# Adaptive modulation in float32 on four column quarters, with key and value products between its tiles

## The reference

```python
silu_c = jax.nn.silu(c)
silu_cc = jax.nn.silu(c_ctx)
shift, scale, gate = jnp.split(silu_c @ w_ada[l] + b_ada[l], 3, axis=-1)
shift_c, scale_c, gate_c = jnp.split(silu_cc @ w_ada[l] + b_ada[l], 3, axis=-1)
h = _modulate(_rmsnorm(xs, norm_g[l]), shift[:, None], scale[:, None])
hc = _modulate(_rmsnorm(cs, norm_g[l]), shift_c, scale_c)
pc_kv = hc @ w_l[:, OFF_K:OFF_ZA]
kc = _rmsnorm(_heads(pc_kv, 0, N_KV_HEADS), k_norm_g[l])
vc = _heads(pc_kv, KV_W, N_KV_HEADS)
p = h @ w_l
q = _rope(_rmsnorm(_heads(p, OFF_Q, N_Q_HEADS), q_norm_g[l]), cos, sin) * q_scale
k = _rope(_rmsnorm(_heads(p, OFF_K, N_KV_HEADS), k_norm_g[l]), cos, sin)
v = _heads(p, OFF_V, N_KV_HEADS)
```

## Time and profile before

| | us |
|---|---|
| Median of 3 runs (2142.15 to 2145.62) | 2142.19 |
| The profiled execution | 2143.34 |
| its span | 2141.70 |
| TensorE busy in the span | 2080.9 |
| VectorE busy | 1376.2 |
| ScalarE busy | 1093.9 |
| GpSimd busy | 48.8 |
| Granted TensorE clock, mean share | 0.987 |

### The profile page before, as it was taken

One profiled execution on the slowest core, in us unless ns is written; L12 is line 12 of the kernel. 1 busy time (PEld: TensorE's weight loads), 2 busy tenths in 40 slices (PEclk: granted clock), 3 DMA queues, 4 the chain that ended last, 5 costly groups with the idle time before them and its releaser, 6 DMA issues.

```text
span 2141.7 us, 30864 instructions
## 1 busy us (share of the span) xinstructions
PE 2080.9 (97%) x12240; PEld 1817.9 (85%) x12240; DVE 1376.2 (64%) x1788; ACT 1093.9 (51%) x1461; POOL 48.8 (2%) x59
## 2 busy tenths in 40 slices
PE   6999999999999998999999999999999999999998
PEld 4678888878889987999998788888789889997886
DVE  4755765557776656666676666666775755775554
ACT  7633455544443444444457666666455445774432
POOL 0000000000000000000000000010000000000000
PEclk9999999999999999999999999999999999999998
DMA  8852443347775554344455445445444454334552
GB/s 352 348 216 99 179 156 119 118 138 275 276 293 178 198 211 153 136 185 178 171 201 193 158 177 193 179 179 201 183 161 175 157 195 177 118 107 168 199 195 79
DMA packets 57802, 394.59 MB, mean 184 GB/s; under 512 B 6624, under 2 KB 9104, under 8 KB 10592
## 3 DMA queue, kind: packets, MB, share of 16 engines
q1 hardware_dynamic: 54240, 376.07, 48.2%
q0 software_dynamic: 2448, 15.51, 1.9%
q10 hardware_dynamic: 1008, 1.53, 0.2%
HBM read 390.92 MB, written 2.16 MB: 184 GB/s over the span
## 4 chain that ended last, share of the span: by engine, by line
PE 93%; DVE 3%; ACT 1%; DMA 1%; issue 1%; SPq 0%; DVEq 0%; ACTq 0%
PE ps L2156 13%; PE ps L2158 13%; PE ps L2157 13%; PE ps L2176 10%; PE ps L2168 9%; PE ps L2170 9%; PE ps L2169 9%; PE ps L2177 5%; PE ps L2265 1%; PE ps L2429 1%; PE ps L2407 1%; PE ps L2256 1%; PE ps L2257 1%; DMA side<-in_ctx 1%; PE ps L2616 1%
## 5 line engine op out<-in xcount | busy, mean ns | idle before, releaser
L1163 DVE TENSOR_TENSOR w_lo<-raw,w_hi 128x1024 fp32r<-128x1024 f32 (+1 forms) x660 | 795.0, 1220 | 569.1 <-ACT w_hi L489 567.4
L489 ACT ACTIVATE w_hi<-raw 128x1024 fp32r<-128x1024 f32 (+1 forms) x660 | 685.3, 1051 | 670.5 <-PE ps L2158 339.0
L2168 PE MATMUL ps<-act,w_hi 128*128 128x256 f32 x1152 | 333.3, 289 | 1.9 <-DVE w_lo L1163 1.2
L2170 PE MATMUL ps<-act,w_lo 128*128 128x256 f32 x1152 | 326.8, 284 | 0.0
L2169 PE MATMUL ps<-act,w_hi 128*128 128x256 f32 x1152 | 326.8, 284 | 0.0
L2176 PE MATMUL ps<-act,w_hi 128*128 128x512 f32 x896 | 315.2, 397 | 1.3 <-DVE side L1438 1.3
L2156 PE MATMUL ps<-w_hi,act 128*128 128x512 f32 (+1 forms) x640 | 252.1, 394 | 4.7 <-DVE act L1206 2.8
L2177 PE MATMUL ps<-act,w_lo 128*128 128x256 f32 x896 | 250.2, 279 | 0.0
L2158 PE MATMUL ps<-w_hi,act 128*128 128x512 f32 (+1 forms) x640 | 247.7, 387 | 0.0
L2157 PE MATMUL ps<-w_lo,act 128*128 128x512 f32 (+1 forms) x640 | 247.3, 386 | 0.0
L2156 PE MATMUL ps<-w_hi,gated 128*128 128x512 f32 x576 | 226.2, 393 | 2.3 <-DVE gated L1978 1.4
(11 more groups left out here) (317 smaller groups left out, 2810.8 us busy)
## 6 DMA issues: line engine op xcount, KB each, us to landing
raw<-in_tiles SPq DMA_DIRECT2D x350, 1024.0 KB, 4.8
gatedf<-acs_dram POOLq DMA_DIRECT2D x8, 1024.0 KB, 7.7
raw<-in_tiles SPq DMA_DIRECT2D x4, 672.0 KB, 4.5
x<-in_x SPq DMA_DIRECT2D x2, 1024.0 KB, 11.0
side<-in_ctx SPq DMA_DIRECT2D x2, 1024.0 KB, 14.7
side<-in_ln_g POOLq DMA_DIRECT2D x2, 1024.0 KB, 6.2
side<-in_ln_b POOLq DMA_DIRECT2D x2, 1024.0 KB, 10.3
out_dram<-x SPq DMA_DIRECT2D x8, 256.0 KB, 2.5
```

What stands on the lines that cost most here:

```text
L489: e.activation(w_hi[:, nth(u) % SPLIT, :, :w], raw[:, t % RAW, 2 * h:2 * h + 2, :w], ACT.Copy).then_inc(hi_done, 1)
L1163: e.tensor_tensor(w_lo[:, slot, :, :w], raw[:, t % RAW, 2 * h:2 * h + 2, :w], w_hi[:, slot, :, :w].bitcast(F32), ALU.subtract).then_inc(lo ...
L2168: e.matmul(o, wh, hi, start=first and f % 2 == 0, stop=False, skip_group_check=True)
L2170: ins = e.matmul(o, wl, hi, start=False, stop=last and f % 2 == 1, skip_group_check=True)
```

## The change

- **Modulation tiles** are no longer split: all 32 are used as float32 (`unsplit` is true for each). The four chunks of a tile go to four column quarters of the array: `cols` has 32 columns a chunk (two not zero), and chunk c writes PSUM partitions 32c to 32c+31 of bank 6. The 192 fast matmuls of 128x512 and the 32 float32 ones become 128 float32 matmuls with 32 weight columns. The four partial sums are added where the rows are turned into columns: `turn_rows` now contracts over 128 partitions instead of 4.
- **Blocks.** A block now holds shift and scale for 256 features, so that each block makes two feature chunks of h ready. Eight blocks of four modulation tiles, each followed by one tile that holds the key and the value weights of those 256 features (`kv`).
- **Order on TensorE.** Transposes first, then block by block; the key steps (`keys`, 12 matmuls each) and value pieces (`value`, 6 matmuls for 128 tokens each) of a block run between the modulation tiles of the next. The separate value block goes.
- **Values** are summed over the blocks in SBUF: VectorE copies the first piece and adds the others (32 operations of 128x512), in place of four ScalarE copies.
- **Loads.** x and ctx are loaded ahead of all weight tiles.
- **Other engines.** VectorE normalises the tokens and copies half of the transposed ones; ScalarE copies the modulation rows and computes the high part straight from scale and shift; affine and low parts are of 256 and 512 columns. The last addition of each of the eight ropes moves to GpSimd. Keys are normalised beside the first query block. Some semaphore increments in later stages are dropped.

The diff, cut to its core:

```diff
-ADA_ORDER = (0, 4, 1, 5, 2, 6, 3, 7)
-ADA_KEYS = ((), (), (), (), (), (0,), (), (1, 2, 3))
...
-    for b, after in zip(ADA_ORDER, ADA_KEYS):
+    for p in range(8):
         for j in range(4):
-            tiles.append(("ada", b, j, CB))
-        for j in after:
-            tiles.append(("key", 0, j, CB))
-    for b in range(1, 10):
+            tiles.append(("ada", p, j, CB))
+        tiles.append(("kv", p, 0, CB))
+    for b in range(2, 10):
         for j in range(4):
             tiles.append(("in", b, j, CB))
...
-        if seg == "key":
-            return rows(a["w_in"], k0, COL_K)
+        if seg == "kv":
+            got = np.stack([a["w_in"][256 * b:256 * b + 256, o:o + CB] for o in (COL_K, COL_V)])
+            return got.reshape(4, P, CB).transpose(1, 0, 2)
         if seg == "ada":
...
 def unsplit(tile):
 
-    return tile[0] == "ada" and tile[2] == 3
+    return tile[0] == "ada"
...
+            for t in range(TT):
+                sp.dma_start(x[:, t, :], a["x"][t * P:(t + 1) * P, :]).then_inc(S["rows_in"], 16)
+            for t in range(TT):
+                sp.dma_start(side[:, t * D:(t + 1) * D],
+                             a["ctx"][t * P:(t + 1) * P, :]).then_inc(S["ctx_in"], 16)
             for n in range(FIRST["gate_a"]):
-                if n == 2:
-                    for t in range(TT):
-                        sp.dma_start(x[:, t, :], a["x"][t * P:(t + 1) * P, :]).then_inc(S["rows_in"], 16)
-                    for t in range(TT):
-                        sp.dma_start(side[:, t * D:(t + 1) * D],
-                                     a["ctx"][t * P:(t + 1) * P, :]).then_inc(S["ctx_in"], 16)
                 load(n)
...
+            def ada_rows(p):
+                e.wait_ge(unsplit_used, 4 * p + 4)
+                o = ROWS + 512 * (p % 2)
+                e.activation(actf[:, o:o + 512], ps[:, 6, :], ACT.Copy).then_inc(act_freed, 1)
+
+            def h_high(p, v):
+                e.wait_ge(S["mod_ready"], p + 1)
+                e.wait_ge(*((S["c_copied"], p // 2 + 1) if v else (S["h_copied"], p // 2 + 1)))
+                for c in range(2 * p, 2 * p + 2):
+                    t = (HI2 if v else LO) + c * 256
+                    e.activation((gated if v else act)[:, 0, c, :], gatedf[:, t:t + 256], ACT.Identity,
+                                 scale=mod[:, 2 * v, c:c + 1], bias=mod[:, 2 * v + 1, c:c + 1]).then_inc(S["h_hi"], 1)
+
+            KV = [n for n, t in enumerate(TILES) if t[0] == "kv"]
...
+            for p in range(8):
+                ada_rows(p)
+                split(2 * KV[p])
+                h_high(p, 0)
+                h_high(p, 1)
+                split(2 * KV[p] + 1)
+                if p == 4:
...
+            def normalise(n):
+                e.tensor_scalar(gatedf[:, n * D:(n + 1) * D] if n < 2 else side[:, (n - 2) * D:(n - 1) * D],
+                                x[:, n, :] if n < 2 else side[:, (n - 2) * D:(n - 1) * D],
+                                sm[:, 44 + n:45 + n], None, ALU.mult).then_inc(S["xn_ready"], 1)
...
+            def affine(p, v):
+                e.wait_ge(S["mod_ready"], p + 1)
+                e.wait_ge(*((S["c_copied"], p // 2 + 1) if v else (S["h_copied"], p // 2 + 1)))
+                for c in range(2):
+                    o = v * 512 + c * 256
+                    t = (HI2 if v else LO) + (2 * p + c) * 256
+                    e.tensor_scalar(side[:, o:o + 256], gatedf[:, t:t + 256],
+                                    mod[:, 2 * v, 2 * p + c:2 * p + c + 1], mod[:, 2 * v + 1, 2 * p + c:2 * p + c + 1],
+                                    ALU.mult, ALU.add).then_inc(S["mod_step"], 1)
+
+            def h_low(p, v):
+                n = 4 * p + 2 * v + 2
+                e.wait_ge(S["mod_step"], 6 * p + 4 + 2 * v)
+                e.wait_ge(S["h_hi"], n)
+                low(side[:, v * 512:v * 512 + 512], gated if v else act, 2 * p, 2).then_inc(S["h_lo"], 1)
+
+            def value(p, tt):
+                n = 4 * p + tt
+                bank = 4 + (tt if p == 7 else n % 2)
+                v = gatedf[:, LO2 + 2048 + tt * 512:LO2 + 2560 + tt * 512]
+                e.wait_ge(*((units_used, nth(2 * KV[p] + 1) + 1) if tt == 3 else (S["v_part"], 3 * p + tt + 1)))
+                if p == 0:
+                    e.tensor_copy(v, ps[:, bank, :]).then_inc(S["v_added"], 1)
+                else:
+                    e.wait_ge(S["v_added"], n - 3)
+                    e.tensor_tensor(v, ps[:, bank, :], v, ALU.add).then_inc(S["v_added"], 1)
+
...
+            for p in range(8):
+                if p:
+                    value(p - 1, 0)
+                modulate(p)
+                split(2 * KV[p])
+                if p:
+                    value(p - 1, 1)
+                affine(p, 0)
+                h_low(p, 0)
+                affine(p, 1)
+                h_low(p, 1)
+                if p:
+                    value(p - 1, 2)
+                    value(p - 1, 3)
+                split(2 * KV[p] + 1)
+            splits(2 * FIRST["in"], 2)
+            for tt in range(4):
+                value(7, tt)
...
+            for n in range(8):
+                b, tt = n // 2, n % 2
+                o = LO2 + tt * 512 if b == 0 else HI2 + tt * 1536 + (b - 1) * 512
+                e.wait_ge(S["rope_step"], ROPE_AT[n])
+                e.tensor_tensor(gatedf[:, o:o + 512], gatedf[:, o:o + 512],
+                                side[:, 1024 + (n % 2) * 512:1536 + (n % 2) * 512], ALU.add).then_inc(S["rope_sum"], 1)
...
-            def modulation(p, m0, n):
-
-                for m in range(m0, m0 + n):
-                    def body(c, slot, m=m):
-                        kc = 2 * m + c
-                        e.matmul(ps[:, 4 + p % 2, :], cols[:, kc, :], w_hi[:, slot, c, :], start=kc == 0, stop=False)
-                        return e.matmul(ps[:, 4 + p % 2, :], cols[:, kc, :], w_lo[:, slot, c, :], start=False, stop=False)
-                    unit(2 * ADA[p] + m, 0, 0, body)
-
-            def modulation_rest(p):
-
-                t = ADA[p] + 3
+            cols = gatedf[:, LO2:LO2 + 512].rearrange("p (k m) -> p k m", m=32)
+
+            def modulation(p, j):
+
+                t = ADA[p] + j
                 e.wait_ge(raw_landed[t % RAW], landed(t))
+                if j == 0 and p:
...
-                                   start=False, stop=c == 3)
+                    ins = e.matmul(ps[32 * c:32 * c + 32, 6, :], cols[:, 4 * j + c, :], raw[:, t % RAW, c, :],
+                                   start=j == 0, stop=j == 3, skip_group_check=True)
                 ins.then_inc(unsplit_used, 1)
...
+            def keys(p, c):
+
+                if p == 0 and c == 0:
+                    e.wait_ge(S["h_copied"], 4)
+                    e.wait_ge(S["c_copied"], 4)
+                e.wait_ge(S["h_lo"], 2 * p + 2)
+                u = 2 * KV[p]
+                e.wait_ge(lo_done, lows(u) + 1)
+                kc = 2 * p + c
+                ins = tokens_out([0, 1, 2, 3], [h_at(kc, tt) for tt in range(4)], kc, nth(u) % SPLIT, c, kc == 0, kc == 15)
+                if c == 1:
+                    ins.then_inc(units_used, 1)
+
+            def value(p, tt):
+
+                u = 2 * KV[p] + 1
+                n = 4 * p + tt
+                e.wait_ge(lo_done, lows(u) + 1)
+                if p == 7:
+                    e.wait_ge(S["v_added"], 28)
+                elif n >= 2:
+                    e.wait_ge(S["v_added"], n - 1)
+                for c in range(2):
+                    ins = tokens_out([4 + (tt if p == 7 else n % 2)], [h_at(2 * p + c, tt)], 2 * p + c, nth(u) % SPLIT, c,
+                                     c == 0, c == 1)
+                ins.then_inc(units_used if tt == 3 else S["v_part"], 1)
+
+            e.wait_ge(S["silu_c"], 2)
             ADA = [n for n, t in enumerate(TILES) if t[0] == "ada" and t[2] == 0]
-            KEY = [n for n, t in enumerate(TILES) if t[0] == "key"]
-            assert BI["ada"] == 0 and ADA[5] == 20 and KEY[0] == 24
...
+            for p in range(1, 8):
+                modulation(p, 0)
+                if p >= 2:
+                    value(p - 2, 2)
+                    value(p - 2, 3)
+                modulation(p, 1)
+                keys(p - 1, 0)
+                modulation(p, 2)
+                keys(p - 1, 1)
+                modulation(p, 3)
+                value(p - 1, 0)
+                turn_rows(p)
+                value(p - 1, 1)
+            value(6, 2)
+            value(6, 3)
```

413 lines of the change are left out of this document (128 added, 285 removed).

## The result

The changed kernel took **2108.68 us** (median of 4, 2107.77 to 2109.49) against 2142.34 for the kernel before (4 runs): a ratio of 0.9837, 95% interval 0.9826 to 0.9849. The forecast was 2100.7, range 2090 to 2126. The sign and the range held. The gain is 33.7 us where 41.5 were forecast.

A forecast was written before the change was run, and what follows sets the result against it. TensorE, busy 97% of the span, was taken as the bound. Its terms to the first query product sum to 163.5 us against 205.5; 2143.34 - 42.0 + 0.5 = 2101.8, less 1.15 to the median: 2100.7, range 2090 to 2126.

The forecast's parts named there:

- The price of a tile: Modulation on TensorE: four float32 column quarters run together at nearly full overlap, 0.90 us a tile, 28.8 us for 32.
- two-deep: Rival, modulation tiles: a second pass holds back the next quarter's first, 1.72 us a tile, 2123.7; chance 0.14 with uncovered loads.
- uncovered-load: Rival, modulation tiles: weight loads between quarters aren't covered, 1.84 us a tile, 2127.5; chance 0.14 together with quarters two deep.
- serial: Rival, modulation tiles: quarters run one after the other, 3.43 us a tile, 2178.5 us, slower; chance 0.12.
- the estimate of 1.08 us: Modulation tile price from the skill's 2.38 times for three column tiles, carried to 3.17 for four; 5.8 us more in the sum.
- slow and half clock: Start of the modulation: TensorE's first 4.9 us run at the slow step, 2.5 us more.
- waits: TensorE before the first query product: first rows 0.9, block 1's tile 1.4, first keys 1.4, last keys 1.2, ring 1.8; 6.7 us.
- Some 60 such changes cost 6.0 us: TensorE in the modulation: each change between 128-wide work and quarter tiles costs about 0.1 us.
- I allow 0.3 a block: Ring of four raw tiles: TensorE waits 0.3 us a block for the fourth modulation tile, 1.8 us in all.
- A wait of 0 to 1.5 us, I take 0.5: First query block: TensorE waits for VectorE's splits, as key normalisation now falls there; 0.5 us added.
- The ring holds: Rival, raw tile ring in the modulation: slow landings cost 2.8 us more in each of six blocks, 2117.5; chance 0.10.
- nothing waits: Rival, up to the first query product: no gaps and waits, 12.7 us less, 2088; chance 0.03.

The follow-up runs named there:

- experiment 6: Changed kernel with the four chunks of a modulation tile on two column quarters, or all on one: 2136.36 us and 2187.59 us.
- experiment 7: Changed kernel with modulation tiles taken two by two, so TensorE changes form four times a block instead of eight: 2105.84 us.
- Experiment 5: Changed kernel with GpSimd's rope additions left out and replaced by two memsets each, which only write: 2104.88 us.
- experiment 4: Kernel before, with the eight rope additions moved to GpSimd (and a semaphore increment dropped in a later stage): 2143.36 us, ratio 0.9999.
- experiment 3: Changed kernel with rope additions back on VectorE and splits for the second and third query block moved ahead of the preceding rope: 2105.93 us.
- experiment 9: Changed kernel with tiles two by two, table loads in block 7, rope additions on VectorE and splits ahead of the rope: 2101.82 us.
- experiment 2: Changed kernel, GpSimd additions kept, with ScalarE's and VectorE's splits for the second and third query block ahead of the preceding rope: 2108.12 us.
- experiment 10: Kernel before in its own tile and instruction order, with all modulation in float32 through four column quarters: 2138.0 us.

## Why the prediction was right or wrong

**The price of a tile: right.** The step that decided (0.90 us for four float32 quarters, read from two row halves) measured 0.88 from tile to tile, 0.86 without the changes of form. The two-deep, uncovered-load and serial rivals are out by experiment 6, and the estimate of 1.08 us worked out from the Trainium skill (TensorE: Matmul & The Clock Gate, Part 3: Packing small matmuls) with them.

**Up to the first query product: 163.5 forecast, 166.0 measured.** By terms, forecast and measured:

| term | forecast | measured |
|---|---|---|
| start of the transposes | 17.7 | 17.5 |
| slow and half clock | 2.5 | 1.4 + 3.1 |
| key and value products | 87.0 | 87.0 |
| modulation, turning rows and the changes of form | 28.8 + 7.8 + 6.0 = 42.6 | 45.8 |
| transposes | 7.0 | 7.3 |
| waits | 6.7 | 4.2 |
| sum | 163.5 | 166.3 |

The measured column is worked out from the traces: 32 tiles at 1.20 less 1.0 for the three pairs that follow one another, 37.4, and eight turnings at 1.05, which is what is left of a block (16.71 less 48 x 0.2265 less 4 x 1.20), 8.4; the first 32 transposes took 5.0 us where the next took 3.65; 6.21 us busy at half clock cost 3.1. The step that failed is "Some 60 such changes cost 6.0 us": going into a tile and out costs 0.34, not 0.2, so 29 times there and back are 9.9 us; the tile itself, at 0.86 instead of 0.90, gives 1.3 back. The clock term lacked the half clock behind the 2.0 us wait of the second block, which lasted 6.8 us here and in experiment 7, and 3.4 in the seven other kernels that have this wait. The waits were overrated: "I allow 0.3 a block" for the ring measured 0.65 in all, once, and its cause was ScalarE's table loads, which the forecast had nowhere. These errors of +3.2, +2.0 and -2.5 partly cancelled.

**Behind it: the step that failed.** "A wait of 0 to 1.5 us, I take 0.5" measured 5.1. The forecast took the eight rope additions off VectorE's account for nothing. Its bound for them asked how long they take on GpSimd (0.6 to 1.6 us by the earlier trace rows; they take 2.2), not what GpSimd does to VectorE meanwhile. VectorE saved 0.69 and lost 1.1 each time, in the one stretch where its cover had been taken away by key normalisation. Not all of the 4.6 us are the additions' own: they act together with splits that stand too late in VectorE's order, and 1.6 are half clock that need not have followed, which is bad luck. Experiment 5 shows the step as the forecast had meant it (88.5 us), with the late splits left as they are, experiment 4 that the kernel before would have hidden it, experiment 3 that it can be given back in full. The row that should have warned was in the forecast's reach: a low part reads two operands from SBUF, the addition does too, and the Trainium skill (SBUF — State Buffer, Who interferes with whom) says what follows.

**Against the rivals.** "The ring holds" came true once in a small form, a wait of 0.65 us in the changed kernel and 2.3 with the tiles two by two; "nothing waits" is what experiment 9 comes near to, at 2101.8 where that rival said 2088, since the changes of form stay.

## What to carry to other kernels

Four float32 matmuls with 32 weight columns ran here in the time of one by quarters, at a fixed price for each change of form, so keep such tiles in pairs, and put them between work that leaves the DMA time to keep up. Before a VectorE instruction is moved to GpSimd, look at what VectorE runs next: if both read two SBUF operands, the move can cost more than it saves, and it shows only where VectorE has no idle time. A wait of 2 us on TensorE can be worth more than 2 us, as half clock may follow; since it may also not, look at the clock of a stretch before two of its times are compared.

## What the runs showed of the hardware

- Four float32 128x512 matmuls on four column quarters: starts 7 ns apart, 0.88 us the four, against 3.43 one after the other; weight loads from the same rows are covered.
- Change of form between full-width products and quarters: 0.34 us for both ways, whatever stands between (2, 4 or 8 passes).
- VectorE and GpSimd take turns when both read SBUF with two operands: a low part takes 2.31 instead of 1.22 us, an addition 2.20 instead of 1.28. A 128x4 TENSOR_SCALAR with one input beside such an addition took 0.77 instead of 0.17. Memsets of 0.31 us on GpSimd cost low parts nothing that shows.
- Half clock in the changed kernel and its variants: behind a wait of 2.0 to 2.5 us in the second block always (nine kernels, for 3.4 or 6.8 us); behind one of 1.9 us in the query stretch in four kernels of six; behind one of 1.9 us in the key transposes in one of them all (experiment 2); never behind waits of 0.3 to 1.5. In experiment 10, where TensorE had waited again and again, it began behind waits of 1.1 to 1.6. The length of the wait alone doesn't tell.
